# A hybrid decoder layer on eight cores: four more weight buffers, other PSUM banks for the sample group, and a pipelined GLA chunk loop

## What is computed

```python
h = x + W_out(sig(gA) * Wa(GLA(xn)) + sig(gB) * Wb(Pool(xn)))   # xn = rmsnorm(x)
h = h + CrossAttn(rmsnorm(h), K_mem, V_mem)                     # 4 heads, 256 memory tokens
h = h + W_down(relu(W_up rmsnorm(h))**2)                        # width 1024 -> 4096 -> 1024
y = rmsnorm(h)
```

## Time and profile before

| | |
|---|---|
| median of 6 runs | 1475.67 us (1474.22 to 1478.29) |
| the profiled execution, and its span | 1479.77 us, 1478.1 us (core 7) |
| TensorE matmul busy | 1333.4 us (90%), 7848 matmuls |
| VectorE, ScalarE, GpSimd busy | 642.9, 518.7, 178.5 us |
| DMA | 261.39 MB, mean 177 GB/s |
| chain that ended last | PE 69%, DMA 20%, DVE 3%, ACT 3%, issue 3% |

### The profile page before, as it was taken

The page is one execution under the profiler, slowest core; times in us unless marked ns, Lnnn a source line. Parts: engine busy times, 40 slices in busy tenths (PEclk is TensorE's granted clock), DMA queues, the critical chain, the costliest instruction groups (busy, mean ns, idle before and its releaser), DMA issues.

```text
span 1478.1 us, 21765 instructions; the slowest of 8 cores (1443.9 to 1478.1 us)
## 1 busy us (share of the span) xinstructions
PE 1333.4 (90%) x7848; PEld 655.6 (44%) x7848; DVE 642.9 (43%) x1137; ACT 518.7 (35%) x1011; POOL 178.5 (12%) x238
## 2 busy tenths in 40 slices
PE   4987979899988989999988999989989899999996
PEld 1444434444434534444433555444444454444442
DVE  2551223544544323545655533453444532353444
ACT  2452224722144413732225531651203441372111
POOL 2231101201102100200000200110011220010000
PEclk9999989999989999999998999999999999999998
DMA  9969999789999599677996316537387996511331
GB/s 202 169 120 193 181 188 173 212 152 194 192 239 173 151 241 266 192 186 216 249 314 244 104 70 219 148 95 229 109 209 182 240 220 164 209 47 50 132 133 64
DMA packets 46949, 261.39 MB, mean 177 GB/s; under 512 B 6038, under 2 KB 6494, under 8 KB 23148
## 3 DMA queue, kind: packets, MB, share of 16 engines
q0 software_dynamic: 16320, 91.68, 38.5%
q1 hardware_dynamic: 30524, 168.33, 32.9%
HBM read 296.02 MB, written 56.36 MB: 238 GB/s over the span
## 4 chain that ended last, share of the span: by engine, by line
PE 69%; DMA 20%; DVE 3%; ACT 3%; issue 3%; POOL 1%; SPq 1%; DVEq 0%; ACTq 0%; POOLq 0%
PE pb L740 63%; PE pb L751 3%; DMA wt_43<-wu 3%; DMA wt_46<-wu 3%; PE pb L770 2%; DMA meml<-mem 2%; DMA sgs<-s0f_84 1%; DMA sps<-tmp_94 1%; PE pb L761 1%; DMA s0f_85<-sgla 1%; DMA yp<-xh 1%; DMA wt_44<-wu 1%; DMA va_144<-cv 1%; DMA sgs<-s0f_85 1%; DMA kv_137<-ckT 1%
## 5 line engine op out<-in xcount | busy, mean ns | idle before, releaser
L817 DVE SCALAR_TENSOR_TENSOR xh<-pb,r_172,xh 128x512 f32<-128x512 f32 x128 | 95.9, 751 | 108.2 <-PE pb L740 107.6
L794 ACT ACTIVATE tmp_92<-pb 128x512 f32<-128x512 f32 (+2 forms) x66 | 38.8, 588 | 213.6 <-PE pb L740 165.1
L806 POOL TENSOR_TENSOR stat<-stat,ncols 128x1 f32<-128x1 f32 (+2 forms) x71 | 47.8, 674 | 540.4 <-DVE stat L812 535.6
L740 PE MATMUL pb<-actT,wt_44 128*128 128x512 bf16 (+2 forms) x440 | 95.6, 372 | 6.4 <-ACT tmp_94 L794 4.2
L740 PE MATMUL pb<-actT,wt_43 128*128 128x512 bf16 (+2 forms) x376 | 84.8, 377 | 16.8 <-DMA wt_43<-wu 13.9
L740 PE MATMUL pb<-actT,wt_46 128*128 128x512 bf16 (+2 forms) x408 | 89.3, 371 | 9.7 <-DMA wt_46<-wu 5.1
L794 ACT ACTIVATE tmp_94<-pb 128x512 f32<-128x512 f32 (+2 forms) x67 | 39.4, 589 | 130.9 <-PE pb L740 69.0
L740 PE MATMUL pb<-actT,wt_45 128*128 128x512 bf16 (+2 forms) x344 | 73.2, 368 | 4.9 <-DVE stat L812 1.7
L740 PE MATMUL pb<-actT,wt_47 128*128 128x512 bf16 x320 | 71.8, 379 | 0.7 <-DMA wt_47<-wscratch 0.7
L794 ACT ACTIVATE tmp_93<-pb 128x512 f32<-128x512 f32 (+2 forms) x58 | 34.0, 587 | 99.5 <-PE pb L740 84.0
L740 PE MATMUL pb<-wt_44,actT 128*128 128x512 bf16 x256 | 62.2, 389 | 5.6 <-DMA wt_44<-wu 3.2
(11 more groups left out here) (507 smaller groups left out, 2345.3 us busy)
## 6 DMA issues: line engine op xcount, KB each, us to landing
wt_45<-wscratch SPq DMA_DIRECT2D x19, 1024.0 KB
wt_43<-wu POOLq DMA_DIRECT2D x17, 1024.0 KB, 17.9
wt_46<-wscratch SPq DMA_DIRECT2D x17, 1024.0 KB
wt_44<-wscratch SPq DMA_DIRECT2D x17, 1024.0 KB
wt_47<-wu POOLq DMA_DIRECT2D x15, 1024.0 KB, 15.7
wt_47<-wscratch SPq DMA_DIRECT2D x14, 1024.0 KB
wt_44<-wu POOLq DMA_DIRECT2D x13, 1024.0 KB, 18.9
wt_46<-wu POOLq DMA_DIRECT2D x13, 1024.0 KB, 18.9
```

Source lines behind the costliest of these rows:

```text
L740: ins = e.matmul(out, l, r, start=(start and i == 0), stop=(stop and i == m - 1))
L794: return self.g.op("act", lambda e: e.activation(out=out, in_=in_, func=func, scale=scale, **kw), reads=rd, writes=wr, cost=c, tab=tab)
L806: return self.g.op(eng, lambda e: e.tensor_tensor(out=out, in0=in0, in1=in1, op=op), reads=[in0, in1], writes=[out], cost=self.vcost(eng, ...
L817: return self.g.op(eng, lambda e: e.scalar_tensor_tensor(out=out, in0=in0, scalar=scalar, in1=in1, op0=op0, op1=op1), reads=rd, writes=[ou ...
```

## The change

Cut to its core (the rest is renumbering):

```diff
 def schedule(self, window=600, margin=1.2):           # PE only
+    for p, i in sorted(now_h[e]):                     # head = first operation not yet listed
+        w = ops[i].ready + (0.0 if p == head else margin)
+        if w <= t: pick = (p, i); break
...
-                dma_free = s + o.nb * 1.08
-                o.end = dma_free + 1.8
+                dma_free = s + o.nb * 1.2
+                o.end = dma_free + 2.0
...
+EARLY = tuple(f"up{i}" for i in range(8)) + tuple(f"dn{c}_{n}" for c in range(4) for n in range(2))
...
+        self.wt += [g.sb(f"wx{i}", g.byname[n] + o, [128, 8, 512], BF16)
+                    for i, (n, o) in enumerate((("WqK", 0), ("WqK", 8192), ("VWo", 0), ("VWo", 8192)))]
...
 def bank(self):
+        a = self.aux                                  # set inside hook() and step()
+        lo, n = (5, 3) if a else (0, 5)
...
-        elif times == 0 or (times == 1 and name[:2] != "up"):
-            cast, store = True, times == 1 or name[:2] == "up"
+        elif times == 0 or (times == 1 and name not in EARLY):
+            cast, store = True, times == 1 or name in EARLY
...
 def program(self):
+        self.act(self.gzs[:, :], self.zero[:16, :], AF.Exp)
+        for i in range(16):
+            self.mm(self.pb[b][:64, :64], [(self.zero[:, :], self.zero[:, :])] * 6)
...
         for c in range(4):
...
+            if c == 0:
+                scores_kdt(0)                         # scores and transposed keys of a chunk
             ogp(1, c, ogb)
             (state update of chunk c)
+            if c < 3:
+                scores_kdt(c + 1)
             (output of chunk c)
...
-  (C_, 3), (X_, 0), (PT_, 1), (X_, 1), (PT_, 2), (M_, 0), (X_, 2), (PT_, 3), (M_, 1), (X_, 3), (M_, 2)
+  (C_, 3), (PT_, 1), (X_, 0), (PT_, 2), (X_, 1), (M_, 0), (PT_, 3), (X_, 2), (M_, 1), (X_, 3), (M_, 2)
...
 def precompute(self):
-        self.dma("sp", self.meml[:, :, :], I["mem"].rearrange("(a p) d -> p a d", p=128))
-        self.dma("sp", self.pmf[:, :], I["wpmT"][:, :])
+        self.dma("pool", self.pmf[:, :], I["wpmT"][:, :], ahead=1e6)
+        self.dma("pool", self.meml[:, :, :], I["mem"].rearrange("(a p) d -> p a d", p=128), ahead=1e6)
```

More of the change, by code:

```diff
@@ L98, in blk_of, with op @@
         return a
-    def op(self, eng, fn, reads=(), writes=(), cost=0.1, dma=False, nb=0, rtok=(), wtok=(), tab=None, ahead=None):
+    def op(self, eng, fn, reads=(), writes=(), cost=0.1, dma=False, nb=0, rtok=(), wtok=(), tab=None, ahead=None, after=()):
         i = self.n
@@ L108, in op @@
         deps = {}
+        for j in after:
+            deps[j] = 0
         if ahead is not None:
@@ L705, in W @@
         if cast:
-            self.dma("pool", flat, src, nb=5.0, ahead=60.0)
+            self.dma("pool", flat, src, nb=5.0, ahead=60.0, after=self.xld[2:3] if k == 1 else self.xld[3:4] if 2 <= k < 9 else ())
         else:
@@ L840, in scan, with dma @@
                          reads=[d0, d1], writes=[out], cost=0.13 + 0.0021 * self.nfree(out))
-    def dma(self, q, out, in_, nb=None, rtok=(), wtok=(), ahead=30.0):
+    def dma(self, q, out, in_, nb=None, rtok=(), wtok=(), ahead=30.0, after=()):
         if nb is None:
@@ L846, in dma @@
         return self.g.op(q, lambda e: e.dma_start(out=out, in_=in_), reads=[in_], writes=[out],
-                         cost=0.6 if q == "pool" else 0.07, dma=True, nb=nb, rtok=rtok, wtok=wtok, ahead=ahead)
+                         cost=0.6 if q == "pool" else 0.07, dma=True, nb=nb, rtok=rtok, wtok=wtok, ahead=ahead, after=after)
     def col(self, name, j=0, n=1, P=128):
@@ L1054, in tile, with scores_kdt @@
         pend = None
-        for c in range(4):
+        ak = {}
+        def scores_kdt(c):
             cs = slice(c * 128, (c + 1) * 128)
-            ogb = self.ring("ogs", self.ogs)
             att = self.ring("att", self.att)
             kdt = self.ring("kdt", self.kdt)
[L1060 to L1063, removed]
-                self.tt("pool", Sb[:, :, :], self.S[:, :, :], pv.unsqueeze(2).to_broadcast([128, 4, 256]), ALU.mult)
-            ogp(0, c, ogb)
             b = self.bank()
@@ L1072, in tile @@
             self.cp("act", kdt[:, :], self.pbf[b][:, :512])
+            ak[c] = (att, kdt)
+        for c in range(4):
+            cs = slice(c * 128, (c + 1) * 128)
+            ogb = self.ring("ogs", self.ogs)
+            have = not (first and c == 0)
+            pv = prv[:, :, 3] if c == 0 else cur[:, :, c - 1]
+            if have:
+                Sb = self.ring("Sb", self.Sb)
+                self.tt("pool", Sb[:, :, :], self.S[:, :, :], pv.unsqueeze(2).to_broadcast([128, 4, 256]), ALU.mult)
+            ogp(0, c, ogb)
+            if c == 0:
+                scores_kdt(0)
             ogp(1, c, ogb)
+            att, kdt = ak[c]
             for hp in range(2):
@@ L1275, in up @@
                     M_(3)
-                    for m in range(3):
+                    hb.append(self.bank())
+                    self.mm(self.pb[hb[3]][:, :384], self.fm(u, 3, A, 384))
+                    for m in range(4):
                         b = hb[m]
@@ L1298, in down @@
                     self.stt("dve", xs, self.pb[b][:, :], rs3[s][:, 0:1], xs, ALU.mult, ALU.add)
-                if each is not None:
+                    if final and c == 3 and s == 3:
+                        st = st if n else self.st4()
+                        self.act(self.xn[n][:, :512], xs, AF.Square, scale=1.0 / 32, accum=st[:, n:n + 1])
+                if final and c == 3 and s == 3:
+                    self.stt("dve", st[:, 2:3], st[:, 0:1], EPS, st[:, 1:2], ALU.add, ALU.add)
+                    self.tt("pool", st[:, 2:3], st[:, 2:3], self.ncols[:, 8:9], ALU.pow)
+                    for n in range(2):
+                        xs = self.xh[:, s, n * 512:(n + 1) * 512]
+                        self.stt("dve", xs, xs, st[:, 2:3], self.gfin[:, n * 512:(n + 1) * 512], ALU.mult, ALU.mult)
+                        self.dma("sp", O["yp"][SEQ - 128:SEQ, n * 512:(n + 1) * 512], xs)
+                elif each is not None:
                     each(s)
                 if s % 2 == 0:
-                    self.step("G")
+                    self.step("G", 2)
                 self.step("K")
-            self.hook("dn", c, ud)
+            if c < 3:
+                self.hook("dn", c, ud)
         def nxt(s):
@@ L1360, in precompute @@
             yield
+        for s in range(2):
+            xn = self.norm_rows(self.meml[:, s, :], dst=self.Mtm[0][:, s, :])
+            self.transT(xn, self.memT, s, "g_mem")
+        yield
         for wh, (nm, on) in enumerate((("xk", "mk"), ("xv", "mv"))):
@@ L1569, in states @@
                            [(qw[:, h, 60 - ST * i:124 - ST * i], sb_[:, h, :])]) for h in (2 * hp, 2 * hp + 1)], i == SB - 1)
-            for hp in range(2):
                 b = self.bank()
```

102 lines of the change are left out of this document (67 added, 35 removed).

## The result

The changed kernel takes 1434.09 us at the median, the kernel before, beside it, 1476.93; the ratio is 0.9707 (95% interval 0.9691 to 0.9722). Medians and spans can hold executions in which a die was disturbed; the ratios leave those out. The forecast was 1431 us and "faster".

What follows compares the result with a forecast made beforehand. DMA casts and stores were taken to set the pace up to tile 1's O, PE with holes behind it. Terms -4 - 24 - 10 - 6 - 1 = -45 gave 1434.8, at the median 1431 us; range 1395 to 1463.

Steps and rivals of the forecast that it cites:

- case A: The prediction's own sum for the whole kernel: 1431 us, own range 1415 to 1446; chance 0.45.
- Front: Up to tile 1's O: early down stores and planner's DMA cost together -4 us, bounds +25.6 and -22.
- The first step: Eight more stores in tile 0: tile 1's k unit lands 3 us later, 23 of 28 idle DMA us used.
- The second step: Planner's higher DMA cost per cast takes back 7 of PE's 19.2 idle us in tile 1's v, chunk and pool.
- Rival C: Most of the early stores' 25.6 us stays: front +20 instead of -4, 1455 us; chance 0.19.
- B: Idle DMA time is used in full: front -22, states -27, 1410 us; chance 0.17.
- Sample states: Tile 1's MLP: eight casts with stores become plain loads, 49 us of DMA time leave, -24 us.
- Rival D: One PSUM bank, pb5, for all state products makes PE wait for DVE: slower, 1497 us; chance 0.11.
- C, X and first up unit: New order, fourth group on 384 columns, one reciprocal for four, cutting PE's waits: -10 us, bounds 0 and -15.
- Chunk loop: GLA scores and transposed keys one chunk ahead remove kdt's wait and some chunk idle time: -6 us, bounds 0 and -16.
- Start: 96 warm-up matmuls before x arrives give 0, since casts set this stage; at most 4 us.
- P: Casts don't bound; four more buffers remove nearly all front idle time: -50 instead of -4, 1385 us; chance 0.05.

Runs made afterwards that it cites:

- e9: The changed kernel itself, run again as a control: ratio 0.9693 to the kernel before, 1437.83 us.
- e3: The changed kernel with PSUM banks given out round robin over all eight, for tile and sample alike: ratio 0.9857.
- e5: The kernel before with one edit, PSUM banks 0 to 4 for the tiles and 5 to 7 for hooked and generator work: ratio 0.9983.
- e1: The changed kernel with all eight down units cast and stored in tile 1, as in the kernel before: ratio 0.9613, 1427.8 us.
- e6: The changed kernel with four of the eight down units cast and stored in tile 1, the other four in tile 0: ratio 0.9627.
- e7: The changed kernel with buffers of their own for the stores of mk, mv and sps, instead of the tmp buffers: ratio 0.9645.
- e11: The changed kernel with one step of the sample states per whole sequence, and one step where two were taken: ratio 0.9688.
- e8: The changed kernel with the old order of C and X, three groups on 384 columns and one reciprocal per row: ratio 0.9782.
- e10: The changed kernel with scores and transposed keys of a GLA chunk made in that chunk again: ratio 0.9660.
- e4: The changed kernel with the planner of the kernel before, without margin and with its old DMA costs: ratio 0.9761.

## Why the prediction was right, and where its sum was not

The forecast of 1431 us was met within 0.3%, and its case A drew the right picture of the result: nothing in the front, the gain behind it. That the number came so close is luck: the sum held errors of some 21 us one way and 23 the other.

**Front, forecast -4, measured +4.0, and +10.6 in the control.** The first step, +3, held by its time: k had landed by 421.8 us (forecast 427), and tile 1's v began at 402.3 for 401.0. It did not hold by its reason. 23 of 28 idle DMA microseconds were to be used; chunk (1.02) and X (0.87 for 0.71) did use theirs, but pool idled as much anew, and 4 of the 28 were used in all (16 in the control, e9, whose share is 0.97). With shared banks (e3) it is 20: 0.02 x 387.8 = 8 us are left idle. So the split banks, to which the sum gave no price in the front, hold up tile 0, in the kernel before (e5) too.

The second step failed: "I take 7 of these back" in tile 1's v, chunk and pool, which took 175.0 us for 172.3. The debt of the eight stores falls due mostly there: by e1 17.9 of the 24.0 us that the early units cost the front, by e6 half of the units cost 10.0. Rival C's mechanism was thus at work, with the price that C gave it, and most of B's gain beside it (e1's front, without the early units, is 20.0 us shorter than before; B had 22); the prediction had them as alternatives to A, and the result is their sum. "Tile 0's O before 220 us" failed too (231.1), through waits that no term named: without those for the stores of mk and mv it is 226.0 (e7), with shared banks 222.9 (e3), and neither shortens the front.

**Sample states, forecast -24, measured -21.2** (tile 1's MLP to tile 2's O, 268.6 to 247.4 us). The size held, and most of the reason. The prediction gave the gain to 49 us of DMA time, and sgs and s0f did leave the chain of waits. With those 49 us put back (e1) they return to it, and the stretch takes 16.2 us more, though all of it behind the MLP. With the banks shared again (e3) it takes 14.0 us more, but holds 56 more weight loads. At e3's 251.04/1528 = 0.164 us of PE per matmul that is, by an estimate, 9 us of work that stands elsewhere in the changed kernel; the next stretch, up to tile 3's v, is 9.3 us shorter. Some 5 us are left for the banks. First the changed kernel, then e1, then e3:

```profile
655.30:902.70 247.40, 239.85 (x1446) 114.28 (x1471) 132.51 (x252) 82.02 (x157) 17.20 (x16) 1.00 0.54 189
```

```profile
632.20:895.80 263.60, 248.06 (x1480) 115.91 (x1479) 132.41 (x255) 82.87 (x158) 20.41 (x22) 0.98 0.66 200
```

```profile
651.20:912.60 261.40, 251.04 (x1528) 120.51 (x1527) 134.94 (x259) 87.23 (x164) 17.25 (x16) 0.99 0.54 182
```

**Rival D is refuted.** One bank for all state products: in the changed kernel no wait of PE in tile 1's MLP is longer than 0.2 us, e11 finds the finer steps without effect, and e3 shows that the separation which D feared was the most valuable edit of all, 24 us by the ratio. The sum had no term for it. It shows where nothing was forecast, in tile 3: v to X, with nearly equal work, takes 18.7 us less than before, and 32.9 us more when the banks are shared again. By e5 it pays only with the rest of the change. By the rule that the prediction cited to make D dearer, of the Trainium skill's page "TensorE: Matmul & The Clock Gate", section on psum-queue depth-cycling, cycling through the banks costs PE its clock. The runs here do not decide it: tile 3's v to pool has a clock of 0.94 in e3 and of 0.99 in the kernel before, and both give the banks out round robin over all eight.

**C, X and first up unit, forecast -10:** the four X stages became 4.2, 1.7, 0.4 and 3.5 us shorter, together 9.8; e8, undoing it, costs 13 us by the ratio. Right.

**Chunk loop, forecast -6: 0 in the rest, and probably a loss in the front** (e10). The step that failed is "That removes the wait for kdt ... and part of the chunk stages' idle time": with the old loop the rest is as long. That the planner fills the time with other work either way was e10's rival; it fits, but is not shown.

**Tail -1: right** (-1.2). **Start 0: right for the warm-up**, though tile 0's chunk began 4.0 us earlier (58.2 for 62.2). The warm-up matmuls did not keep the clock: behind them 8 transposes took 0.89 us, the next 8, after a wait for x, 1.01; the 31 recorded matmuls of v0 took 9.48 us, the next 31 7.08. That is what the rule of the Trainium skill's page "TensorE: Matmul & The Clock Gate", section on HAM oscillation, had said of idle stretches. What made the start shorter is that PE used v0's cast at 21.65 us, where it was 30.17.

```profile
1.40 5.26 PE L775 MATMUL pb<-zero 128*64 128x64 bf16 x96 [1.40 <-DVE ncols L864]
9.72 0.89 PE L805 MATMUL pb<-ident,xn_100 128*128 128x128 bf16 x8 [3.06 <-DVE xn_100 L847]
14.90 1.01 PE L805 MATMUL pb<-ident,xn_101 128*128 128x128 bf16 x8 [4.29 <-DVE stat L847]
...
21.65 9.48 PE L775 MATMUL pb<-wt_43,actT 128*128 128x512 bf16 x31 [1.22 <-DMA wt_43<-wu]
...
34.73 7.08 PE L775 MATMUL pb<-wt_44,actT 128*128 128x512 bf16 x31
```

**P and B** are out as the whole result: casts and stores still bound tile 0's MLP and tile 1's v and chunk, at DMA shares of 1.01 to 1.02, and the front gained nothing.

So, against the forecast, the front came 12 us worse (8, and tile 0's X stage, whose 4.2 us stand under C and X), the chunk loop 6 and the states 3, 21 us together. Some 23 us were not in the sum: 18.8 in tile 3 (351.4 us to its last matmul became 329.1, X aside) and most of the rest in tile 2 behind its pool. The split banks alone (e5) gave 11.3 in tile 3. Of the planner's 10 us (e4) the prediction had 7, in the wrong place.

**Still open:** why split banks hold up tile 0, in the kernel before (e5) as in the changed one (e3); which waits they remove in tile 3; why e6 and e7 do not combine; why the chunk loop costs front time.

## What to carry to other kernels

Split the kernel at the last point where transfers set the pace, and compare front and rest apart: in the rest 3 us were told from nothing by one execution, in the front not even 7. A store moved out of a late stage into one that is full was paid there at nearly its whole length, in part a stage later than it stands; half of the early stores (e6) beat all of them by 10 us, and none of them (e1) by 12. Giving background work PSUM banks of its own was worth more (24 us) than any of the waits named in the profile before, but only together with the rest of the change, and at a price in tile 0. When an edit moves work between stages, compare stretches with equal counts of weight loads, not stages.

## What the runs showed that was not expected

- The cores differ most in the front. In the kernel before it ended between 545.4 (core 0) and 573.3 us (core 7), in the changed one between 568.4 (core 0) and 577.3 (core 6): the slowest core lost 4.0 us there, the fastest 23. The rest took 880 to 893 us before and 840 to 843 in the changed kernel. The spans of the changed kernel's fastest and slowest core:

```profile
core 0: 1420.8 us, clock 0.974
...
core 6: 1430.6 us, clock 0.968
```

- Small stores hold a queue for long: of two sets of 16 stores of sps (the sample's pool state), SP needed 6.83 us to issue the first and 19.98 us for the second (6.34 and 9.56 in the kernel before), behind which the next stores of weights waited.

```profile
487.29 6.83 SPq L881 DMA_DIRECT2D sps<-tmp_98  x16
494.20 0.36 SPq L881 DMA_DIRECT2D wscratch<-wt_47  x1
494.65 19.98 SPq L881 DMA_DIRECT2D sps<-tmp_99  x16
```

- A transfer that is worth 3.2 us by bandwidth took 38.94 us from issue to landing, with the DMA share at 1.02: the queue's length, not the transfer's, is what a buffer waits for.
